# Memory attention taken into the branch merge; the SSD branch's gate, squares and group norm moved out of the memory attention stage

## The reference, cut to what matters

```python
# h: (1, 1024, 1024); one layer; all float32
proj = rms_norm(h, norm_mix_pre) @ w_in
sb_qkv, z, xbc_raw, dt_raw, mem_q, gate_logits = split(proj)
y_sb  = stick_breaking_attention(q, k, v)                     # 16 heads of 64
y     = ssd_chunked(...) + d * xh                             # 4 groups, 32 heads, chunks of 128 tokens
y     = y * silu(z)                                           # the SSD gate
yg    = y by group of 512 channels                            # 4 groups
y_ssd = yg * rsqrt(mean(yg * yg) + EPS) * ssd_norm            # group norm
k, v  = split(rms_norm(mem) @ w_mem_kv)                       # 256 memory rows
y_mem = softmax(q_mem @ k.T / 16) @ v                         # 4 heads of 256
merged = (sigmoid(g0) * (y_sb @ w_sb_out) + sigmoid(g1) * (y_ssd @ w_ssd_out)
          + sigmoid(g2) * (y_mem @ w_mem_out))                # 1024x1024 each
h = h + rms_norm(merged @ w_o); then a squared-ReLU MLP
```

## Time and profile before

| | |
|---|---|
| Time, median of 3 runs (lowest, highest) | 3107.1 us (3106.19 to 3108.37) |
| The profiled execution's own time, its span | 3107.75 us, 3106.0 us |
| Busy share of the span: PE, PEld, DVE, ACT, POOL | 90%, 74%, 49%, 30%, 42% |
| Mean granted TensorE clock | 0.953 |
| HBM read, written | 251.26 MB, 95.03 MB |

### The profile page before, as it was taken

How to read it: one execution, slowest core, us unless ns; L and a number is a source line. 1 busy time by engine, 2 the same in 40 slices (tenths; PEclk the granted TensorE clock), 3 DMA queues, 4 the chain that set the end, 5 groups by cost and what they waited for, 6 DMA issues and landing times. The chain is left out here.

```text
span 3106.0 us, 34232 instructions
## 1 busy us (share of the span) xinstructions
PE 2806.8 (90%) x13220; PEld 2313.0 (74%) x13220; DVE 1531.6 (49%) x1574; ACT 934.9 (30%) x1634; POOL 1294.9 (42%) x669
## 2 busy tenths in 40 slices
PE   6999899999999997999975547999987999999997
PEld 4888688888888876877863336777876888888886
DVE  4100067667676666777755553333254434443443
ACT  3101044444444445556543332111032100110002
POOL 5466354445445434545530004434301644543452
PEclk9999999999999998999997778999998999999999
DMA  3354343233342415556445334332231111111112
GB/s 131 126 181 144 103 120 116 96 116 102 115 116 95 122 48 156 164 154 186 146 126 199 133 135 186 140 135 95 74 136 68 63 53 48 54 45 44 48 64 99
DMA packets 151054, 348.27 MB, mean 112 GB/s; under 512 B 14336, under 2 KB 74368, under 8 KB 150912
## 3 DMA queue, kind: packets, MB, share of 16 engines
q1 hardware_dynamic: 150912, 346.34, 33.9%
HBM read 251.26 MB, written 95.03 MB: 111 GB/s over the span
## 5 line engine op out<-in xcount | busy, mean ns | idle before, releaser
L952 POOL TENSOR_TENSOR sb_beta<-sb_beta,sb_rest 128x128 f32<-128x128 f32 (+7 forms) x128 | 163.9, 1280 | 381.4 <-DVE sb_rest L1008 381.4
L790 PE MATMUL sb_psg<-uh,sb_wh 128*128 128x512 f32 x768 | 307.1, 400 | 13.1 <-POOL sb_wl L938 13.1
L790 PE MATMUL sb_psg<-uh,sb_wl 128*128 128x512 f32 x768 | 313.4, 408 | 0.0
L790 PE MATMUL sb_psg<-ul,sb_wh 128*128 128x512 f32 x768 | 306.9, 400 | 0.0
L2127 POOL TENSOR_TENSOR ff_uph<-ff_w,one 128x1024 fp32r<-128x1024 f32 x32 | 61.6, 1924 | 460.0 <-PE ff_ps L2147 320.0
L1788 PE MATMUL mg_ps<-mg_yh,mg_wh 128*128 128x512 f32 x512 | 204.5, 399 | 52.3 <-POOL mg_wl L179 31.6
L172 POOL TENSOR_TENSOR mg_wh<-mg_w,one 128x1024 fp32r<-128x1024 f32 x32 | 62.4, 1950 | 453.5 <-DMA mg_w<-in_w_branch 284.2
L1008 DVE TENSOR_TENSOR_SCAN sb_rest<-sb_rest 128x128 f32<-128x128 f32 (+7 forms) x128 | 181.4, 1417 | 138.1 <-ACT sb_rest L900 137.3
L2147 PE MATMUL ff_ps<-vh,ff_uph 128*128 128x512 f32 x512 | 200.3, 391 | 12.8 <-POOL ff_upl L2130 12.8
L2162 PE MATMUL ff_psd<-ff_dnh,ff_fh 128*128 128x512 f32 x512 | 199.8, 390 | 4.8 <-issue 4.8
L2216 DVE TENSOR_TENSOR ff_total<-ff_psd,ff_total 128x1024 f32<-128x1024 f32 x112 | 136.8, 1222 | 133.5 <-PE ff_psd L2162 133.5
(11 more groups left out here) (277 smaller groups left out, 7244.3 us busy)
## 6 DMA issues: line engine op xcount, KB each, us to landing
sb_w<-in_w_in SPq DMA_DIRECT2D x48, 512.0 KB, 5.0
scratch_proj<-sb_out SPq DMA_DIRECT2D x48, 512.0 KB, 3.0
sb_k<-scratch_qk SPq DMA_DIRECT2D x64, 256.0 KB, 6.3
ssd_arow<-scratch_decay SPq DMA_DIRECT2D x32, 512.0 KB, 5.5
mg_raw<-scratch_y SPq DMA_DIRECT2D x32, 512.0 KB, 6.2
mg_w<-in_w_branch SPq DMA_DIRECT2D x32, 512.0 KB, 4.6
mg_gate<-scratch_proj SPq DMA_DIRECT2D x32, 512.0 KB, 3.5
ff_w<-in_w_up SPq DMA_DIRECT2D x32, 512.0 KB, 3.6
```

The lines of the kernel that those rows point to most:

```text
L790: last = nc.tensor.matmul(ps_g[:, h], l[:, s, k], r[:, k, h * HALF:(h + 1) * HALF], start=(k == 0 and j == 0), stop=(k == KB - 1 and j == 2))
L952: nc.gpsimd.tensor_tensor(beta[:, i % 3, 0:cols], beta[:, i % 3, 0:cols], rest[:, i % 3, 0:cols], ALU.mult).then_inc(weighted, 1)
```

## The change

1. The stage `memory_attention` is gone. Its attention runs inside `merge_branches`, which is now written as 64 slots of 24 block matmuls each (5.4 us at the rate of the kernel before). Each head is cut into two units of four steps; a unit has a period of five slots, the first in slot 5, the last ending in slot 46. PE does a step's transposes and scores ahead of the slot's block matmuls; the transposes of a step stand one slot behind its scores. Scores, exponentials and transposed probabilities have one buffer each in place of two.
2. The eight y blocks of a part are no longer split ahead of it: the first two output blocks of a part are done two input blocks at a time over four slots, and the splits of the next part run from the last slot of the part before. The raw y buffer is a ring of five blocks. The part with the memory branch is the last.
3. In the SSD stage POOL multiplies y by silu(z) (a new load, `load_z`), ACT squares it at the end of an iteration, behind `evacuate(2n+1)`, and POOL adds the four blocks' squares in two steps (`fold_squares`) at the end of its own iteration; SP stores the 128x128 sum (`squares`).
4. In the merge, PE sums those squares over the partitions (eight matmuls in place of 32), ACT takes the root, DVE inverts it, and `normalize` multiplies each y block in the merge's buffer.
5. Additions to `merged` move from DVE to POOL; the clearing of `merged` is gone.

```diff
 # ssd
+            def load_z(n):
+                if n >= 2:
+                    sp.wait_ge(y_done, n - 1)
+                sp.dma_start(zT[:, n % 2], src).then_inc(z_loaded[n % 2], 16)
...
+            def square_of(n):                       # ACT, last in iteration n + 2
+                act.wait_ge(y_done, n + 1)
+                if n:
+                    act.wait_ge(folded, n)
+                nc.scalar.activation(sq[:], yT[:, n % 2], ACT.Square).then_inc(squared, 1)
...
+            def fold_squares(n):                    # POOL, last in iteration n + 2
+                pool.wait_ge(squared, n + 1)
+                if n:
+                    pool.wait_ge(sq_stored, 16 * n)
+                nc.gpsimd.tensor_tensor(part_sq[:], sq[:, 0:2], sq[:, 2:4], ALU.add).then_inc(folded, 1)
+                pool.wait_ge(folded, n + 1)
+                nc.gpsimd.tensor_tensor(part_sq[:, 0], part_sq[:, 0], part_sq[:, 1], ALU.add).then_inc(sq_done, 1)
...
                     pool.wait_ge(summed, 2 * n)
-                    nc.gpsimd.tensor_tensor(yT[:, 1 - b], yT[:, 1 - b], skip[:, 1 - b], ALU.add).then_inc(y_done, 1)
+                    nc.gpsimd.tensor_tensor(yT[:, 1 - b], yT[:, 1 - b], skip[:, 1 - b], ALU.add).then_inc(skipped, 1)
+                    pool.wait_ge(skipped, n)
+                    pool.wait_ge(z_loaded[1 - b], 16 * ((n - 1) // 2 + 1))
+                    nc.gpsimd.tensor_tensor(yT[:, 1 - b], yT[:, 1 - b], zT[:, 1 - b], ALU.mult).then_inc(y_done, 1)
+                if n >= 2:
+                    fold_squares(n - 2)
...
 # merge_branches
+    RAW, W_RAW, W_KEPT = 5, 2, 3
+    UNITS, STEPS, PERIOD, MA0 = 2 * MEM_HEADS, 4, 5, 5
+    STAT_AT = (7, 9, 20, 24)                        # slots of the four groups' square sums, two slots each
...
+        def split_slot(kk):
+            return kk // KB * PART - 1 + kk % KB // 2
+        def norm_slot(kk):
+            k, begin = kk % KB, kk // KB * PART
+            return begin - 6 + k if k < 4 else begin + (-1, 1, 1, 2)[k - 4]
+        def sigmoid_slot(n):
+            p, i = n // KB, n % KB // 2
+            return p * PART + (2, 6, 9, 13)[i]
...
+            for slot in range(SLOTS):               # PE
+                u, j = memory_step(slot)
+                if u is not None:
+                    if u and j < 2:
+                        weigh_values(u - 1, j)
+                    if u < UNITS:
+                        if j:
+                            turn(u, j - 1)
+                        if j < STEPS:
+                            score(u, j)
+                        if j == 3 and u % 2 == 0:
+                            turn_values(u // 2)
+                for g in range(GROUPS):
+                    if slot in (STAT_AT[g], STAT_AT[g] + 1):
+                        sum_squares(g, slot - STAT_AT[g])
+                p, i = divmod(slot, PART)
+                if i < 4:
+                    two_blocks(p * KB, i)
+                else:
+                    n, h = slot // 2, slot % 2
+                    if h == 0:
+                        begin(n)
+                    last = passes(n, range(KB), (h,))
```

More of the change, by code:

```diff
@@ new lines, in merge_branches @@
+        gate = sb("gate", [P, 2, S])
+        ssq, rstd, gain = sb("ssq", [P, S]), sb("rstd", [P, 2, S]), sb("gain", [P, GROUPS * GB])
+        qT, kT, vT = sb("qT", [P, DB, HALF]), sb("kT", [P, DB, M]), sb("vT", [P, DB, M])
+        qh, ql = sb("qh", [P, DB, HALF], F32R), sb("ql", [P, DB, HALF], F32R)
+        kh, kl = sb("kh", [P, DB, M], F32R), sb("kl", [P, DB, M], F32R)
+        vh, vl = sb("vh", [P, MB, M], F32R), sb("vl", [P, MB, M], F32R)
+        top, less, total, share = (sb(n, [P, 2]) for n in ("top", "less", "total", "share"))
@@ new lines, in merge_branches, with memory_step @@
+        v_loaded, v_turned, v_hi, v_split = (sem(n) for n in ("vld", "vturned", "vhi", "vsplit"))
+        scores, topped, lessened, e_done, inverted, prob_done = (
+            sem(n) for n in ("scores", "topped", "less", "e", "inverted", "prob"))
+        turned, pt_hi, pt_split, y_mm, y_out = (sem(n) for n in ("turned", "pthi", "ptsplit", "ymm", "yout"))
+        stored = sem("stored")
+        def memory_step(slot):
+            return divmod(slot - MA0, PERIOD) if MA0 <= slot < MA0 + UNITS * PERIOD + 2 else (None, None)
@@ new lines, in add @@
+            def add(n):
+                pool.wait_ge(multiplied, n + 1)
+                if n >= 2 * KB:
+                    pool.wait_ge(summed, n - 2 * KB + 1)
+                nc.gpsimd.tensor_tensor(merged[:, n % KB], merged[:, n % KB], gate[:, n % 2], ALU.add).then_inc(summed, 1)
+            for n in range(3):
+                split_w(n)
+            for slot in range(SLOTS + 1):
+                for n in range(KB, N):
+                    if slot == multiply_slot(n):
+                        add(n)
+                for n in range(3, N):
+                    if slot == last_slot(n - 3) + 1:
+                        split_w(n)
@@ new lines, in rest_of_y, with multiply @@
+            def rest_of_y(kk):
+                dve.wait_ge(y_hi, kk + 1)
+                nc.vector.tensor_tensor(yl[:, kk % KB], raw[:, kk % RAW], yh[:, kk % KB].bitcast(F32),
+                                        ALU.subtract).then_inc(y_split, 1)
+            def multiply(n):
+                dve.wait_ge(w_used, n + 1)
+                dve.wait_ge(gate_done, n + 1)
+                out = merged[:, n % KB] if n < KB else gate[:, n % 2]
+                nc.vector.tensor_tensor(out, ps[:, n % 2], gate[:, n % 2], ALU.mult).then_inc(multiplied, 1)
```

691 lines of the change are left out of this document (392 added, 299 removed).

## The result

The changed kernel takes 2971.1 us (median of 4 runs, 2965.6 to 2977.8) against 3107.7 us (3106.2 to 3109.8) for the kernel before on the same chip: ratio 0.9563, 95% interval 0.955 to 0.9576. The forecast was 2985 us. The profiled execution took 2977.78 us, its span is 2976.0 us against 3106.0, and its granted clock 0.969 against 0.953.

A forecast was written before the change was run, and what follows sets the result against it. PE's own stream was taken to set the time nearly everywhere, except the 260.5 us gap between SSD and merge. 3107.75 - 260.5 + 19.9 + 75.1 + 42 + 1.1 = 2985.4, forecast 2985 us, range 2945 to 3030.

The forecast's parts named there:

- The gap goes, a shorter one comes: Between SSD's last matmul and the merge's first: 260.5 us go, 19.9 us come.
- The merge, +75.1: Merge from first matmul to last gate product: 456.2 us against 381.1, from added PE work, slow start and new waits.
- PE's own new waits: PE stalls in the merge's new interleaved slots: 42 us, bounded by 10 below and 90 above.
- The group norm: Eight merge slots with root table change and DVE reciprocal ahead of the next maximum: 2 us each, 16 us.
- The chain of 4.3 us: Merge slot, from a step's scores through `prob` to transposed probabilities: 4.3 us of 6.4, leaving 2 us to spare.
- The part boundaries: Starts of merge parts 1 to 3, with splits and `normalize` on DVE: stalls of 6, 6 and 2 us, 14 us.
- Table changes: Two sigmoids and two table loads ahead of an exponential in about eight merge slots: 1 us each, 8 us.
- PE's added work: Merge: transposes, scores, value products and sums of squares add 63 us to PE; the low-clock first block 3 us.
- SSD, +42: SSD stage: folds waiting for ACT's square delay `xe` and the state, 1.3 us x 32; stores and z loads cause no wait.
- SSD nearly free and slack that holds: Rival: SSD additions cost 10 us and the merge's waits 15, giving 2926 us; chance 0.22.
- DVE and POOL meeting in the slots: Rival: DVE and POOL collide in merge slots far more than counted, waits of 90 us, giving 3033; chance 0.16.
- The SSD loop closed over POOL: Rival: SSD's fold makes one serial ring, slower than before from 5.1 us an iteration, 3119 us at 5.5; chance 0.04.

The follow-up runs named there:

- e5: e4_both with the group norm's reciprocal run twice in each of its 8 places: 2941.9 us, ratio 0.947.
- e6: e4_both with the group norm's reciprocal run three times in each of its 8 places: 2975.6 us, ratio 0.9577.
- e7: e4_both with a copy in place of the sigmoid of the merge's branch gate: 2923.1 us, ratio 0.9414.
- e1: Changed kernel with two buffers for the folded squares instead of one: 2959.8 us, ratio 0.9514.
- e9: Changed kernel, single buffer kept, with the store of the squares issued at the head of SyncE's iteration: 2959.5 us, ratio 0.9533.
- e2: Changed kernel with ScalarE's square moved up behind evacuate(2n), single buffer and fold's place kept: 2952.9 us, ratio 0.9493.
- e10: Changed kernel with two buffers for the folded squares and the early square, fold still ahead of `xe`: 2922.7 us, ratio 0.9415.
- e8: e4_both without GpSimd's product of y with z; z is still loaded: 2926.9 us, ratio 0.9425.
- e4_both: Changed kernel with the square behind evacuate(2n), the fold behind `aged`, and two buffers for the folded squares: 2927.4 us, ratio 0.9409.
- e3: Changed kernel with the fold moved behind `aged`, one iteration later, two buffers, square's place kept: 2929.7 us, ratio 0.9419.
- e11: e4_both with the fold of chunk n-3 straight behind `xe` instead of behind `aged`: 2922.8 us, ratio 0.9413.

## Why the prediction was right, and where it wasn't

*The gap goes, a shorter one comes.* Right: 260.5 went and 21.3 came for 19.9. The first DMA left 12.0 us after SSD's last matmul (10.8 forecast); the row of the fold at 1686.38 has `[1.75 <-DMA scratch_squares<-ssd_psq]`, the same store that was thought free.

*The merge, +75.1.* Measured +48.0; the mis-sized term is "PE's own new waits", 42 us by my count, 9.4 in the trace, just below the lower bound of 10. Its parts:
- The group norm, 16 us forecast: 2.0 for all of `mg_prob`. The chain of 4.3 us and the 2 us to spare were right for plain slots, but I set the 3.35 us of the reciprocal against the 2 us as if nothing ran in between. It starts after `prob` is done and runs while PE is in the slot's rest, so DVE's idle time ahead of the next maximum is cover as well. e5 and e6 show that this cover is nearly used up: 27 us more of the same work cost 15 to 19 us, and 54 cost 48 to 52.
- The part boundaries, 14 us forecast: of the 6.0 us in six waits for `mg_yl`, 1.1 stand in the merge's first 3 us and 4.9 at the starts of parts 1 to 3 (1.9, 2.6 and 0.4 for 6, 6 and 2). The mechanism is there, at a third of the size.
- Table changes, 8 us forecast: at most 0.8, by e7. The 4 us for other meetings with POOL don't show as a wait of their own. 35 loads of 1283 ns were there as counted, in ScalarE's idle time. The Trainium skill's advice to batch calls by table set (ScalarE: Activation LUTs, Table sets: the hidden batching unit) would have gained next to nothing here: 21 loads less, of 35, moved the merge by 0.8 us.
- PE's added work: 63 us and 3 for the slow start were forecast. 429.1 - 348.2 - 9.4 is 71.5 us, 5.5 more. The granted clock of 0.98 over 430 us can carry them: 2% off the clock is about 8.6 us, 3 of which I had in the start. This is an estimate and was not tried by itself.

*SSD, +42.* Measured +59.6 at its end. The step that failed is "The squares' stores and the loads of z cause no wait: each is issued an iteration or nearly so before its reader". For z it held: GpSimd never waits for it. The store was issued 7.0 us before the fold could have used its buffer (1237.21 and 1244.23), less than half an iteration, behind five other DMAs, and it landed 8.8 us later. With this wait gone (e1, e9) the stage is at +43.7 and +44.9, which is my 42 for the ring through ScalarE's square; e2, with that ring gone and the store's left, is at +35.2, and with both gone the stage is at +7.1 (e10). So the mechanism that I named was right in place and in its sum, and a second one beside it, which I had excluded, made the stage 13 to 15 us longer. The spread of the sum was wrong: I gave the iteration without a state "almost none", but without the store's wait (e1) the two iterations around it still take 3.1 to 3.8 us more than before. The gate product was priced at nothing and costs nothing in e8, which was built on e4_both; within the changed kernel itself this was not tried.

*The signs.* As forecast, `xe` is let go by the folds, and `xeh` waits for `xe`, 66.1 us in 26 waits. The iterations that took 15.2 us were to take 16 to 17; six of these eight take 16.6 or 16.7, and two, in which the store decides, 17.7 and 18.3. One so passes the 18 that I had named as a sign of failure. PE's idle time in the merge was to stand at `mg_prob` and the y splits and does, with 2.0 and 6.0 of the 9.4 us. The merge's clock is 0.98, above the 0.95 named.

*The rivals.* SSD nearly free and slack that holds: the second half came true, and e10 shows the whole of it, 2922.7 us where 2926 was worked out, once both waits are out. DVE and POOL meeting in the slots: no; 9.4 us of waits. The SSD loop closed over POOL: it did close, through the fold's two waits, but (58.3 us)/32 is 1.8 us an iteration, far from the 5.1 at which it decides.

*The luck in it.* The errors of +18 and -27 us cancelled: the sum of 2985.4 us is 7.7 off the profiled execution's 2977.8, and the other 6 of the 14 us to the median of 2971 are that execution's place as the slowest of four. The sum was better than its terms. The range was not quite its own: SSD and waits of 20 each make 2941, not 2945.

The remaining 4 to 13 us of SSD in e3, e4, e10 and e11 were not explained.

## What to carry to other kernels

When a small reduction and its store are added to a ring of engines, ask three things of it: which engine's late result it waits for, what stands behind it on its own engine, and what its store stands behind in the DMA queue, waits and transfers both, while its buffer is taken. Here a fold of 1.2 us in each iteration, in the same place, left the stage 58 or 7 us longer by what it waited for, and the cure was a second buffer of 128x256 and an earlier place for the square. When two waits end at the same instruction, price them together, since taking one away gives back only up to the other. Look at the odd iterations too: most of what the late store cost fell where two groups meet. And count as cover for a long operation all idle time of its engine up to its next reader, but across neighbouring slots and not slot by slot.

## What the runs showed of the hardware

- Waits in TensorE's stream cost more than themselves: 10.2 us more of them lengthened the merge by 17.3 us (e5), 32.5 us by 48.1 (e6). The rest is the same matmuls taking longer, with a granted clock of 0.50 behind a wait of 4.5 us and a mean of 0.97 and 0.94 over the merge against 0.99.
- A store of 64 KB took 6.3 us (median) from issue to landing behind five other DMAs of its queue, and 1.6 us at their head (e9).
- A table load on ScalarE took 1283 ns, and it ran as soon as its activation was next in order, ahead of that activation's wait: the load at 1748.68 was over 3 us before DVE's next maximum, for which the exponential waited. Loads in such idle time cost nothing (e7).
- The times of the kernel before drifted between the three groups of runs (medians 3110.0, 3106.2 and 3104.1 us), so differences of 5 us between kernels of different groups were read by their ratios alone.
